# w_in's first 3072 columns as three groups of 1024 columns by eight k-pairs, six of the blocks as seven products, and the first loads in 256 KB pieces

## The reference

```python
h = rms_norm(x, attn_norm)
z = h @ w_in
r_q, r_k, r_v, r_g, c_q, c_kv, k_pe, g_u, g_v = jnp.split(z, IN_SPLITS, axis=-1)
...
x = x + y @ w_out
h = rms_norm(x, ffn_norm)
return x + (jax.nn.silu(h @ w_gate) * (h @ w_up)) @ w_down
```

## Time and profile before

| | us |
|---|---|
| runs before | 1102.52, 1103.56, 1103.9; median 1103.56 |
| profiled execution, its own time | 1103.76 |
| its span (first to last instruction) | 1102.0 |
| PE busy | 1091.2 (99%) |
| DVE busy | 844.1 (77%) |
| ACT busy | 603.1 (55%) |
| DMA | 212.53 MB, mean 193 GB/s |
| granted TensorE clock, mean | 0.999 |

### The profile page before, as it was taken

One profiled execution on the slowest core, in us unless ns is written; L12 is line 12 of the kernel. 1 busy time (PEld: TensorE's weight loads), 2 busy tenths in 40 slices (PEclk: granted clock), 3 DMA queues, 4 the chain that ended last, 5 costly groups with the idle time before them and its releaser, 6 DMA issues.

```text
span 1102.0 us, 13415 instructions
## 1 busy us (share of the span) xinstructions
PE 1091.2 (99%) x5155; PEld 907.4 (82%) x5155; DVE 844.1 (77%) x776; ACT 603.1 (55%) x597; POOL 38.7 (4%) x44
## 2 busy tenths in 40 slices
PE   9999999999999999999999999999999999999997
PEld 6788889997888888888888888888888888888886
DVE  6444457664475788898888888898988899999994
ACT  6644446665655565555555554544655655565553
POOL 0390000000000000000000000000000000000000
PEclk9999999999999999999999999999999999999999
DMA  9755544554355555555556555555555665555552
GB/s 349 260 190 190 191 141 137 191 177 130 123 181 183 167 192 208 206 191 190 195 191 215 198 190 191 196 215 197 190 192 195 229 217 197 192 196 205 208 191 114
DMA packets 58323, 212.53 MB, mean 193 GB/s; under 512 B 4016, under 2 KB 11952, under 8 KB 41008
## 3 DMA queue, kind: packets, MB, share of 16 engines
q1 hardware_dynamic: 56288, 206.58, 54.3%
q10 hardware_dynamic: 2000, 5.46, 1.3%
HBM read 209.93 MB, written 2.10 MB: 192 GB/s over the span
## 4 chain that ended last, share of the span: by engine, by line
PE 96%; ACT 1%; DMA 1%; DVE 1%; issue 0%; ACTq 0%; SPq 0%; DVEq 0%
PE ps L1497 62%; PE ps L1273 9%; PE ps L1275 9%; PE ps L1274 9%; PE ps L1312 2%; DMA raw<-in_w_in 1%; PE ps L1410 1%; PE ps L1360 1%; PE ps L1461 1%; PE ps L1462 1%; PE ps L1463 1%; PE ps L1359 0%; ACT w_hi L409 0%; ACT junk L436 0%; DVE w_lo L816 0%
## 5 line engine op out<-in xcount | busy, mean ns | idle before, releaser
L1497 PE MATMUL ps<-w_hi,xp_hi 128*128 128x512 f32 x539 | 211.7, 393 | 0.0
L1497 PE MATMUL ps<-w_hi,xp_lo 128*128 128x512 f32 x539 | 209.9, 389 | 0.0
L1497 PE MATMUL ps<-w_lo,xp_hi 128*128 128x512 f32 x539 | 209.7, 389 | 0.0
L816 DVE TENSOR_TENSOR w_lo<-raw,w_hi 128x2048 fp32r<-128x2048 f32 (+2 forms) x44 | 91.9, 2088 | 88.9 <-ACT w_hi L409 88.9
L1008 DVE TENSOR_TENSOR w_lo<-raw,w_hi 128x2048 fp32r<-128x2048 f32 x55 | 125.8, 2287 | 36.1 <-ACT w_hi L621 36.1
L621 ACT ACTIVATE w_hi<-raw 128x2048 fp32r<-128x2048 f32 x55 | 105.0, 1909 | 62.2 <-DMA raw<-in_w_gu 62.2
L1273 PE MATMUL ps<-w_hi,xT_hi 128*128 128x512 f32 (+1 forms) x352 | 132.8, 377 | 1.5 <-DVE w_lo L816 1.5
L1275 PE MATMUL ps<-w_hi,xT_lo 128*128 128x512 f32 (+1 forms) x352 | 131.0, 372 | 0.0
L1274 PE MATMUL ps<-w_lo,xT_hi 128*128 128x512 f32 (+1 forms) x352 | 130.9, 372 | 0.0
L710 ACT ACTIVATE w_hi<-raw 128x2048 fp32r<-128x2048 f32 (+1 forms) x44 | 79.2, 1799 | 78.2 <-DMA raw<-in_w_dn 78.2
L1497 PEld LDWEIGHTS ps<-w_hi,xp_lo 128*128 128x128 f32 x539 | 101.2, 188 | 21.4
(11 more groups left out here) (235 smaller groups left out, 1896.9 us busy)
## 6 DMA issues: line engine op xcount, KB each, us to landing
raw<-in_w_gu SPq DMA_DIRECT2D x88, 1024.0 KB, 4.8
raw<-in_w_dn SPq DMA_DIRECT2D x44, 1024.0 KB, 4.8
raw<-in_w_in SPq DMA_DIRECT2D x34, 1024.0 KB, 5.1
raw<-in_w_out SPq DMA_DIRECT2D x16, 1024.0 KB, 5.0
raw<-in_w_in SPq DMA_DIRECT2D x8, 576.0 KB, 3.8
raw<-in_w_ukv SPq DMA_DIRECT2D x3, 1024.0 KB, 5.3
raw<-in_w_uq SPq DMA_DIRECT2D x3, 768.0 KB, 4.4
xT_raw<-in_xT SPq DMA_DIRECT2D x4, 512.0 KB, 8.0
```

What stands on the lines that cost most here:

```text
L816: nc.vector.tensor_tensor(w_lo[n % 4][:, 0:k, 0:c], raw[n % 4][:, 0:k, 0:c], w_hi[n % 4][:, 0:k, 0:c].bitcast(F32), ALU.subtract).then_inc ...
L1497: mm = nc.tensor.matmul(out, x, wt, start=start and j + m == 0, stop=stop and 3 * j + m == n - 1, skip_group_check=resumed)
```

## The change

The 3072 columns become three groups of 1024 columns; a chunk is now one k-pair (256 rows) by 1024 columns, still 1 MB, laid out by the host so that each of 128 partitions reads 8 KB in one row. A group has eight chunks (`FB` = 8) and uses banks 0 to 3. The pairs are taken in the order 0 to 7 in the first group, and 5, 0, 6, 1, 7, 2, 3, 4 in the second and third. There the first, third and fifth chunk (pairs 5, 6, 7) are seven-product blocks of 21 matmuls instead of 24; sums of the activation blocks for these pairs are made once, in the first group. The chunks 24 and up are as before. The loops of ACT, DVE, PE and SP over the groups are written out.

```diff
+IN_ORDER = [list(range(8))] + [[5, 0, 6, 1, 7, 2, 3, 4]] * 2
+IN_SUMS = (5, 6, 7)
+FIRST = (1, 3, 0, 2)
...
+            load_x(0)
+            for j, landed in zip(FIRST, (*first_in, raw_in[0])):
+                sp.dma_start(raw[0][:, j:j + 1, :], w_i3[:, 0:1, j * COLS:(j + 1) * COLS]).then_inc(landed, 16)
+            load_x(1)
+            for j, landed in ((0, half_in), (2, raw_in[1])):
+                sp.dma_start(raw[1][:, j:j + 2, :]..., w_i3[:, 1:2, j * COLS:(j + 2) * COLS]).then_inc(landed, 16)
+            for n in range(2, FB):
+                load_x(n)
+                if n < RING: (load of chunk n)
+            for n in range(RING, C0):
+                load_rows(n, n % 4, w_i3[:, n:n + 1, :])
```

(`load_x(k)` loads 256 KB of x, k-tiles 2k and 2k+1.) ScalarE:

```diff
+            def x_sums_hi(s):
+                act.wait_ge(xi_step, 3 * (s + 1))
+                nc.scalar.activation(xi_hi[s][:], xi[s][:, 4:8, :], ACT.Copy).then_inc(xi_sums_hi, 1)
+
+            def in_hi(n):
+                slot, s = n % 4, in_sum(n)
+                act.wait_ge(raw_in[slot], 16 * (n // 4 + 1))
+                blocks = slice(0, 4) if s is None else slice(1, 4)
+                nc.scalar.activation(w_hi[slot][:, blocks, :], raw[slot][:, blocks, :], ACT.Copy).then_inc(hi_ready, 1)
+                if s is not None:
+                    act.wait_ge(in_sum_step, 3 * (s + 1))
+                    nc.scalar.activation(ti_hi[s % 2][:], ti_sum[s % 2][:], ACT.Copy).then_inc(in_tops_hi, 1)
...
+            for n in range(2, FB):
+                split_x_hi(n)
+                in_hi(n)
+                if n in (3, 4):
+                    act.dma_start(xin[:, n - 3, :], x_v[:, n - 3, :]).then_inc(x_in[n - 3], 16)
+                if n == 5:
...
+                    act.dma_start(decay[:], t["decay"]).then_inc(consts_in, 16)
...
+                if n >= 6:
+                    x_sums_hi(n - 6)
             for b in range(TOK):
                 act.wait_ge(x_in[b], 16)
                 sum_squares(nx, b, junk[:], xin[:, b, :], nx.ss[:, b:b + 1])
             root(nx, 2, D)
...
+            for n in range(FB - AHEAD, C0):
+                g, p = divmod(n, FB)
+                if n + AHEAD < C0:
+                    in_hi(n + AHEAD)
+                if n == FB - AHEAD:
+                    x_sums_hi(2)
+                if g and p == 4:
+                    act.wait_ge(in_mix_done, 2 * (g - 1) + 1)
+                    if g > 1:
+                        act.wait_ge(in_mixed, 2 * (g - 1))
+                    nc.scalar.activation(mix_in[:, 0, :], bank[4], ACT.Copy).then_inc(in_mix_first, 1)
+                if p == FB - 1:
...
+                    for j in range(4):
...
+                            act.wait_ge(in_done, 3 * g + j + 1)
...
+                        nc.scalar.activation(z_ret[:, b, c:c + COLS], bank[j], ACT.Copy, scale=nx.r[:, b:b + 1]).then_inc(acc_free, 1)
+                if n + AHEAD >= C0:
+                    high(n + AHEAD, c=width(n + AHEAD))
```

VectorE (`in_lo`, `in_mix_sums` and `in_mix_banks` do for these chunks what `prep_lo`, `mix_sums` and `mix_banks` do in the FFN; the three block sums are lines 1016 to 1021 on `ti_sum`):

```diff
+            for n in range(2, FB):
+                split_x_lo(n)
+                if n in IN_SUMS:
+                    x_sums(IN_SUMS.index(n))
+                in_lo(n)
+                if n >= 6:
+                    x_sums_lo(n - 6)
+            for n in range(FB - AHEAD, C0):
+                g, p = divmod(n, FB)
+                if g and p == 4:
+                    in_mix_sums(g)
+                    in_mix_banks(g, 0)
+                if g and p == 5:
+                    in_mix_banks(g, 1)
+                if n + AHEAD < C0:
+                    in_lo(n + AHEAD)
+                else:
+                    low(n + AHEAD, c=width(n + AHEAD))
+                if n == FB - AHEAD:
+                    x_sums_lo(2)
+                    invert(nx)
```

TensorE:

```diff
-            keep_warm(24)
+            keep_warm(14)
...
+            def in_sums(n):
...
+                pe_.wait_ge(xi_made, x + 1)
+                pe_.wait_ge(lo_ready, n + 1)
...
+                for out, left, right in ((4, "a11", "b11"), (5, "n2", "t2"), (7, "s1", "t1"), (6, "s3", "t3"),
+                                         (0, "a12", "b21"), (2, "s4", "b22"), (1, "a22", "t4")):
+                    if start and out < 3:
+                        pe_.wait_ge(acc_free, 4 * (g - 1) + out + 1)
...
+                    mm = group(bank[out], [x_hi], [x_lo], [hi], [lo], start, stop and out >= 4)
...
+            def in_plain(n):
...
+                for side in range(4):
+                    half, b = divmod(side, 2)
+                    if g and p == 1 and side == 3:
+                        pe_.wait_ge(acc_free, 4 * g)
+                    if g and p == 6 and b == 0:
+                        pe_.wait_ge(in_mixed, 2 * (g - 1) + half + 1)
+                    mm = in_side(n, b, half, (0, 1), ...)
+                    if g and p == 5 and side == 1:
+                        mm.then_inc(in_part_done, 1)
+                    if p == FB - 1 and side < 3:
+                        mm.then_inc(in_done, 1)
+                mm.then_inc(chunk_used, 1)
```

More of the change, by code:

```diff
@@ L464, in _ @@
-            high_half(1, 2, raw_in[1], hi_ready)
+            for j, landed, made in ((0, half_in, half_hi), (2, raw_in[1], hi_ready)):
+                act.wait_ge(landed, 16)
+                nc.scalar.activation(w_hi[1][:, j:j + 2, :], raw[1][:, j:j + 2, :], ACT.Copy).then_inc(made, 1)
             def evacuate(n, count, dsts, func=ACT.Copy, scale=None, banks=0, out=acc_free):
@@ L486, in _ @@
             root(nx, 2, D)
[L487 to L494, removed]
@@ L914, in _ @@
                         dve.wait_ge(acc_free, ACC_C)
-                        dve.wait_ge(first_free, 2)
                     else:
@@ new lines, in group, with in_side @@
+            def group(out, x_hi, x_lo, w_h, w_l, start, stop, resumed=False):
+                n = 3 * len(x_hi)
+                for j in range(len(x_hi)):
+                    for m, (x, wt) in enumerate(((x_hi[j], w_h[j]), (x_hi[j], w_l[j]), (x_lo[j], w_h[j]))):
+                        mm = nc.tensor.matmul(out, x, wt, start=start and j + m == 0, stop=stop and 3 * j + m == n - 1,
+                                              skip_group_check=resumed)
+                return mm
+            def in_side(n, b, half, kts, start=False, stop=False, resumed=False):
+                slot, pair, toks = n % 4, IN_ORDER[n // FB][n % FB], slice(b * P, (b + 1) * P)
+                blocks = [2 * j + 1 - half for j in kts]
+                return group(bank[2 * half + b], [xT_hi[:, 2 * pair + j, toks] for j in kts],
+                             [xT_lo[:, 2 * pair + j, toks] for j in kts], [w_hi[slot][:, j, :] for j in blocks],
+                             [w_lo[slot][:, j, :] for j in blocks], start, stop, resumed)
@@ new lines, in _ @@
+            for m, j in enumerate(FIRST):
+                if m == 0:
+                    pe_.wait_ge(xT_made, 1)
+                if m < 3:
+                    pe_.wait_ge(first_lo, m + 1)
+                else:
+                    pe_.wait_ge(lo_ready, 1)
+                for b in range(TOK):
+                    mm = in_side(0, b, 1 - j % 2, (j // 2,), start=j < 2)
+            mm.then_inc(chunk_used, 1)
+            pe_.wait_ge(xT_made, 2)
+            for k in range(2):
+                if k == 0:
+                    pe_.wait_ge(half_lo, 1)
+                else:
+                    pe_.wait_ge(lo_ready, 2)
+                for side in range(4):
+                    mm = in_side(1, side % 2, side // 2, (k,))
@@ L1433, in _ @@
+            mm.then_inc(chunk_used, 1)
+            for n in range(2, C0):
+                if in_sum(n) is None:
+                    in_plain(n)
+                else:
+                    in_sums(n)
             pe_.wait_ge(ident_in, 16)
```

288 lines of the change are left out of this document (177 added, 111 removed).

## The result

| | us | ratio to before (95% interval) |
|---|---|---|
| before, median of 4 | 1103.73 | |
| changed, median of 4 (1113.75 to 1116.61) | 1114.21 | 1.0102 (1.009 to 1.0115) |
| forecast | 1110.6 (1102.5 to 1115.5) | |
| changed, profiled execution | 1113.87, span 1112.1 | |

The change makes the kernel 1% slower, 10.5 us. The forecast had the sign, the place and most of the size: 7.0 of the 10.5. The result lies in its range of 1102.5 to 1115.5, but above the 1108 to 1113 that it gave the forecast's own mechanism.

The account below looks back on a forecast made before the run. PE was taken as the bound, busy throughout 55 to 142 us. Removed work -7.8, steady waits +11.3 and moved row work +3.5 gave +7.0 on 1103.76, so 1110.6 for the median, range 1102.5 to 1115.5.

Parts of the forecast that it names:

- the forecast's own mechanism: Bank changes and mixes: PE waits for copies queued behind ScalarE's preparation of chunk n+3; 1108 to 1113, chance 0.52.
- the start and the hole: Before chunk 7: ten fewer warm matmuls start PE earlier, -2.1; the old wait of 1.45 at 43.84 goes, -1.6.
- First bank change: In chunk 8: PE waits for ScalarE's bank copies, 2.9 if ScalarE is on time, plus 3.5 from row work.
- the steady 13.1: PE's time from start of chunk 7 to start of chunk 9 if ScalarE is on time, instead of 10.2.
- ScalarE's row work behind chunk 7: Sums of squares, table and root, moved behind chunk 7, delay the first bank change: +3.5 (bounds 0 and 7).
- Mixes: Chunks 14 and 22: PE waits before both halves for mixes behind ScalarE's late bank 4 copy; 2.35 each, 4.7 together.
- The 0.27: Constant: a PE restart after a wait costs 0.27 more than the wait, from a first matmul of 0.50 against 0.23.
- Second bank change: In chunk 16: same wait for bank copies as the first, with DVE behind by the late mixes; 3.7.
- rival (b): The clock falls after long PE holes, some 3 us each: 1113.6 after one, 1116.6 after two; chance 0.14.
- Matmuls: Six seven-product chunks save three matmuls each of 0.2267 us: -4.08.
- (c): Rival: steady 1 MB loads land in 2.7 us, not 4.8, so waits shrink to 2 to 3; 1098.4, chance 0.08.
- (d): Rival: as many waits, half as long, for instance bank copies coming between parts of in_hi; 7.4, 1103.5, chance 0.10.

Follow-up runs that it names:

- e1: Changed kernel, with ScalarE copying a group's four banks to z_ret before it prepares chunk n+3; 1103.07 us, ratio to before 0.9995.
- e3: Changed kernel with two reorderings on ScalarE: bank copies to z_ret, and bank 4's copy for the mix, both before preparing chunk n+3; 1099.4 us, 0.9966 to before.
- e8: e3 with 24 warm matmuls at the start, as in the kernel before, instead of 14; 1098.95 us, ratio to before 0.9965.
- e11: Changed kernel with ScalarE's two sums of squares over 64 columns of x instead of 2048; 1113.86 us, ratio to before 1.0096.
- e12: e11 with GpSimd's first operation held until chunk 9 is used; 1113.65 us, ratio to before 1.0096.
- e9: Changed kernel with bank copies first and eight products in all 24 chunks, no block sums, no mixing; 1101.68 us, ratio to before 0.9988.
- e4: Changed kernel with 24 and 12 warm matmuls on zeros in front of chunks 8 and 16; 1112.4 us, ratio to before 1.0082.
- e6: Changed kernel with ScalarE's sums of squares moved between w_hi and t_hi of chunk 8, the root behind t_hi; 1115.46 us, ratio to before 1.0111.
- e2: Changed kernel, with ScalarE copying bank 4 to mix_in before it prepares chunk n+3; 1110.95 us, ratio to before 1.0065.

## Why the prediction was right, and where its sizes were off

The mechanism held: PE sets the time here, the bank changes wait for copies that ScalarE makes behind the preparation of chunk n+3, and this costs more than 18 matmuls, the early start and the old hole give. e1 to e3 show it by undoing the order alone: 14.8 us come back, and the sign turns. The signs that the prediction named came as well: holes of 5.9 and 3.0 (forecast 5 and 3) in front of the fifth product of chunks 8 and 16, and holes in front of both halves of chunks 14 and 22. One did not: it allowed no hole beyond 0.5 before chunk 8, and there was one of 0.93 in front of chunk 2.

By its steps, forecast and measured (the latter from S values):

- From S7 before to S7 after (the start and the hole): -3.7 in the sum (-2.1 and -1.6), while the 45.3 for S7 that the later terms use would be -4.1; measured 46.18 - 49.41 = -3.2, in one trace of each, and S7 varies by 1.6 us from trace to trace (e8). The warm matmuls end at 6.97 and not 7.25, but a wait of 0.93 in front of chunk 2 was not in the sum. By the forecast chunk 2 was due at 18.13 (7.25 + 10.88); TensorE starts it at 19.00. These 0.9 are the distance from 45.3 to 46.18. The term counted the start as if nothing behind it could be late; in e8 it was worth nothing that can be measured.
- First bank change, S9 - S7: forecast 16.6 (61.9 - 45.3), measured 18.55. This is the term that was mis-sized, and for the part beyond the steady 13.1 also mis-explained. I gave it to ScalarE's row work behind chunk 7 (3.5). Its chain had only ScalarE in front of the t_hi of chunk 8, but VectorE's block sums for it end at 46.7, only 1 us before ScalarE is there at 47.67. By e11 and e12 the 5.4 beyond the steady value are: row work 0.3 (18.55 to 18.29), GpSimd at the same time as VectorE 2.0 (18.29 to 16.30), the slow clock about 1.1, and some 2.1 left for VectorE's own queue (the sums for chunks 8 and 10 and for x). The last two are what remains by subtraction and the count of slow matmuls, not by a run of their own for this place.
- Mixes, S15 - S12 and S23 - S20 beyond 15.64: forecast 2.35 each, measured 1.81 and 1.79. Places, releasers and chain are as forecast: the copy of bank 4 starts at 87.31, 6.9 after S12 (7.0), and the second mix ends at 95.06, 14.7 after it (15.0). By the matmuls' starts TensorE was late by 1.15 (due 90.72, 91.87) and 0.43 (due 94.68, 95.11), and the first interval behind each restart is some 0.1 longer than 0.23 (91.87 to 92.18 is 0.31), 1.8 in sum. The step that failed is how the constant was used. The 0.27 was read from a duration (0.50), which is not the distance to the next start; yet as something on top of the wait that the profile prints it holds: 0.99 and 0.27 printed, each with 0.27, are 1.8, since a printed wait starts 0.16 after the due time (a record of 0.39 against a distance of 0.23) and 0.1 comes behind it. The prediction put it on top of lateness against the due time, which has the 0.16 in it already. 0.27 in place of 0.1, twice, is 0.34 of the 0.54 too much; the rest is the first lateness, 1.15 and not 1.35.
- Second bank change, S17 - S15: forecast 13.9 (10.2 + 3.7), measured 14.82; the slow clock adds about 1.1 that was only in rival (b), so the wait itself was put 0.2 too high.
- Matmuls: -4.08 by the count. Their net value is 2.3 by the medians and 3.6 between S7 and S24 by the traces (e9 against e3). What the traces miss of 4.08 are the waits for VectorE's t_lo at chunks 8 and 10 that the block sums bring (1.7 with their restarts), less the hole at chunk 8 of e9 (1.2).

In sum at S24: forecast 7.0, measured 9.4. The slow clock (2.2), the rest of the first bank change (0.9) and the start (0.5) are what was too low, 0.1 is the S24 of before, and the mixes (-1.1) and the second wait (-0.2) what was too high. So it is partly luck that the total came as near: the forecast left out the clock, which it had as a rival, and the mixes made up for half of it.

Rival (b) came true together with the forecast and not in its place, with a third of its price. I took the 14 slow matmuls of the start as the price of one hole (3 us); the rows show seven intervals from 61.22 to 64.37, in 3.15 us where 1.7 would be due (7 x 0.227 + 0.1). Of these 1.45 about 0.3 would have gone into a wait for the third bank's copy at full speed, so 1.1 to 1.2 a hole remain (the second change has seven intervals in 3.06, from 109.27 to 112.33), and e4 gives 1.8 for both by the medians. The price is not fixed: behind the second hole of e12 it was 2.7. That it is the clock, the trace shows at both bank changes (0.53 granted behind each), and e4 by its warm matmuls in the holes: 1.00 granted from 60 to 70 and from 108 to 115. (c) and (d) did not happen: the load of chunk 15 lands in 4.8 us (80.71 to 85.49, where ScalarE starts on it), and the copies do wait for the whole of `in_hi`. (By its own terms (d) comes to 1103.2 and not 1103.5; nothing hangs on it.)

## What to carry to other kernels

Work that frees a resource of the bottleneck (an evacuation, the copy that starts a mix) belongs ahead of the work that prepares data three chunks away, on an engine that takes its work in order, as ScalarE did here (banks complete at 51.9, its copies at 60.49, behind the t_hi of 58.68); here its place alone was worth 14.8 us, four to six times the gain of the fewer matmuls. When a wait in front of an engine goes, ask of each wait behind it whether it stands on the same chain: starting PE 1.65 us earlier (e8 against e3) brought nothing that could be measured, with chunk 2 waiting for its w_lo in both. To attribute a wait, take the suspected work away rather than move it: the move in e6 met another wait and told nothing of its cost, and e12 gave back at the second place what it gained at the first.

## What the runs showed of the hardware that was not expected

Operations of VectorE get longer while GpSimd computes. In the changed kernel the same block sum of 128x1024 takes 1.36 instead of 1.22, one of 128x512 up to 0.96 instead of 0.69, and ti_lo up to 2.63 instead of 2.29; with GpSimd delayed (e12) all are back at 1.22, 0.69 and 2.29 in the same place. Once GpSimd has ended in the changed kernel too (busy 4.51 of 10 us from 80 to 90, then 0), they are back at these times from 88 us on. GpSimd's operations get longer too, and by more. The same operation on 128x192 elements takes 0.7 while VectorE is mostly idle and 2.6 beside ti_lo (49.61 to 52.24), as far as GpSimd's spans in a profile, which are rough, can tell:

```profile
47.28 0.69 POOL L410 TENSOR_SCALAR ang_t<-turns 128x192 f32<-128x192 f32 x1
...
50.18 2.61 POOL L410 TENSOR_SCALAR ang_t<-turns 128x192 f32<-128x192 f32 x1
```

By what mechanism, no run here shows. In the changed kernel GpSimd's work adds between nothing (ti_lo at 60.62 takes 2.29 while GpSimd is busy) and 40% (the block sum of 0.96 against 0.69) to an operation of VectorE.

The clock can fall after a hole has ended and PE is busy again: in e4 it fell 1.5 us after a wait of 2.35 us (matmuls 0.43 apart from 94.47 on, granted clock 0.53) and in e2 2.0 us after one of 2.50 (the same from 110.01 on, 0.50), while the holes of 1.0 at the mixes (granted 1.00 from 90 to 97 and from 138 to 146) and the one of 1.45 before (1.00 from 43.8 to 50) left it as it was.
